# Feed-forward output: the last six inner tiles of output tiles 2 to 5 as two pairs of seven products

## What is computed

```python
def rms_norm(x, g):
    y = x * lax.rsqrt(jnp.mean(x * x, axis=-1, keepdims=True) + EPS)
    return y * g

def half_swiglu(x, g, w_in, w_out):
    a, b = jnp.split(rms_norm(x, g) @ w_in, 2, axis=-1)
    return x + 0.5 * ((jax.nn.silu(a) * b) @ w_out)

for i in range(2):
    x = half_swiglu(x, norm_w[i, 0], w_ffn_in[i, 0], w_ffn_out[i, 0])
    x = x + mixer(rms_norm(x, norm_w[i, 1]))     # state space, then attention
    x = half_swiglu(x, norm_w[i, 2], w_ffn_in[i, 1], w_ffn_out[i, 1])
y = rms_norm(x, norm_f)
```

## Time and profile before

| | us |
|---|---|
| median of 3 runs | 2453.65 (2452.84 to 2457.1) |
| the profiled execution, its own time | 2449.32 |
| its span in the trace | 2447.5 |
| PE busy | 2414.4 (99% of the span) |
| DVE busy | 1837.7 (75%) |
| ACT busy | 1392.9 (57%) |
| POOL busy | 755.4 (31%) |

### The profile page before, as it was taken

The page is one execution under the profiler, slowest core; times in us unless marked ns, Lnnn a source line. Parts: engine busy times, 40 slices in busy tenths (PEclk is TensorE's granted clock), DMA queues, the critical chain, the costliest instruction groups (busy, mean ns, idle before and its releaser), DMA issues.

```text
span 2447.5 us, 50261 instructions
## 1 busy us (share of the span) xinstructions
PE 2414.4 (99%) x19713; PEld 2362.0 (97%) x19713; DVE 1837.7 (75%) x3054; ACT 1392.9 (57%) x2388; POOL 755.4 (31%) x739
## 2 busy tenths in 40 slices
PE   8999999999999999999999999999999999999998
PEld 8999999999999989999999999999999998999998
DVE  8979766977777788978876988875235438988875
ACT  7757553545555556757666766664223227767663
POOL 1222224545555542222223222224322321222222
PEclk9999999999999999999999999999999999999999
DMA  6677753133333325676765677764433434677762
GB/s 192 162 170 166 171 118 111 49 103 106 106 106 97 106 83 147 152 177 160 175 139 137 150 172 162 172 148 134 158 131 122 136 110 111 158 172 162 174 149 88
DMA packets 105686, 339.01 MB, mean 139 GB/s; under 512 B 13776, under 2 KB 17360, under 8 KB 87184
## 3 DMA queue, kind: packets, MB, share of 16 engines
q1 hardware_dynamic: 53936, 242.40, 30.0%
q0 software_dynamic: 51552, 93.87, 22.8%
HBM read 223.06 MB, written 19.32 MB: 99 GB/s over the span
## 4 chain that ended last, share of the span: by engine, by line
PE 94%; DVE 4%; ACT 1%; issue 1%; DMA 0%; SPq 0%; POOL 0%; DVEq 0%; ACTq 0%
PE ps L1644 17%; PE ps L1642 17%; PE ps L1652 17%; PE ps L1540 7%; PE ps L1548 7%; PE ps L1541 7%; PE ps L1661 2%; PE ps L1662 2%; PE ps L1669 2%; PE ps L1591 1%; PE ps L1581 1%; PE ps L1582 1%; PE ps L1980 1%; PE ps L1982 1%; PE ps L1981 1%; DVE sb_acc L2713 1%
## 5 line engine op out<-in xcount | busy, mean ns | idle before, releaser
L1644 PE MATMUL ps<-sb_ual,sb_hw 128*128 128x288 f32 x2240 | 614.2, 296 | 0.0
L1642 PE MATMUL ps<-sb_uah,sb_hw 128*128 128x288 f32 x2240 | 610.7, 295 | 0.1
L813 POOL DMA_DIRECT2D sb_lw<-sb_rawf x328 | 282.3, 866 | 961.6 <-ACT sb_lw L987 944.8
L1642 PEld LDWEIGHTS ps<-sb_uah,sb_hw 128*128 128x128 f32 x2240 | 421.0, 188 | 0.7 <-issue 0.5
L1644 PEld LDWEIGHTS ps<-sb_ual,sb_hw 128*128 128x128 f32 x2240 | 421.2, 188 | 0.0
L796 POOL TENSOR_TENSOR sb_wl<-sb_raw,sb_wh 128x512 fp32r<-128x512 f32 (+1 forms) x170 | 282.4, 1678 | 389.8 <-ACT sb_wh L956 377.3
L1652 PE MATMUL ps<-sb_uah,sb_lw 128*128 128x288 f32 x2240 | 385.0, 294 | 0.0
L1540 PE MATMUL ps<-sb_uh,sb_wh 128*128 128x288 f32 x1360 | 373.6, 301 | 0.1
L1541 PE MATMUL ps<-sb_ul,sb_wh 128*128 128x288 f32 x1360 | 366.8, 296 | 0.0
L1652 PEld LDWEIGHTS ps<-sb_uah,sb_lw 128*128 128x128 f32 x2240 | 328.3, 188 | 0.7 <-DVE sb_lw L2336 0.4
L1540 PEld LDWEIGHTS ps<-sb_uh,sb_wh 128*128 128x128 f32 x1360 | 255.7, 188 | 7.6 <-issue 5.0
(11 more groups left out here) (366 smaller groups left out, 5096.3 us busy)
## 6 DMA issues: line engine op xcount, KB each, us to landing
sb_lw<-sb_rawf POOLq DMA_DIRECT2D x358, 256.0 KB, 3.7
sb_rawf<-w_ffn_in SPq DMA_DIRECT2D x87, 1024.0 KB, 5.0
sb_rawf<-w_ffn_so SPq DMA_DIRECT2D x32, 1024.0 KB, 5.0
sb_raw<-w_ssd SPq DMA_DIRECT2D x64, 512.0 KB, 3.6
sb_raw<-w_att SPq DMA_DIRECT2D x40, 512.0 KB, 3.7
sb_rawf<-w_ffn_out SPq DMA_DIRECT2D x32, 384.0 KB, 3.1
sb_h<-state SPq DMA_DIRECT2D x8, 1024.0 KB, 5.1
ssm_sample<-sb_h SPq DMA_DIRECT2D x8, 1024.0 KB, 4.8
```

Of the source, the lines that this page charges most:

```text
L813: pool.dma_start(slot(lw, p), rawf[:, s % 2, i * BL:(i + 1) * BL], accum_op=ALU.add).then_inc(ld_in[i], 16)
L1642: pe.matmul(out, w[:, k * P:(k + 1) * P], high[k], start=begins and k == 0, stop=False, skip_group_check=True)
L1644: pe.matmul(out, w[:, k * P:(k + 1) * P], low[k], start=False, stop=False, skip_group_check=True)
```

## The change

The unit count of a stage grows from 30 to 32: units E0 = 30 and E1 = 31 do the last six inner tiles for the output tiles 2 and 3 (E0) and 4 and 5 (E1) by sevens, with 3 pairs of inner tiles instead of 4, so 9 matmuls a product. The output tiles 0, 1, 6 and 7 stay plain. PE's order is: tiles 0 and 1, the products of E0 and E1, tile 6 (with product 4 of E1 behind its first two blocks), tile 7. The inner tiles 16 to 21 get their sums of halves (`h_side3`, `h_sides`, `high_hs`, `low_hs` with 3 sides of 288 columns, and `high_s4_out`, `low_s4_out` for the fourth). The weights of E0 and E1 come in two transfers of 768 KB. All work on the scaled tiles of the next stage stands behind product 7 of E1 in DVE's list, for the tiles in the order 0, 1, 3, 2, 5, 4, and only then comes `add_out(6)`.

```diff
-NU = 30
+NU = 32
+OUT_TILES = (0, 1, 6, 7)
+END_SLOT = {1: 3, 5: 4, 6: 5, 2: 6, 3: 0, 7: 1, 4: 2}
+LAST = 29
+E0, E1 = 30, 31
+ORDER = (0, 1, 3, 2, 5, 4, 6, 7)
...
+        def tile_done(f, m):
+            if m in OUT_TILES:
+                return x_done, OUTS * f + OUT_TILES.index(m) + 3
+            return x_part, UPDATED[f * NU + E0 + m // 2 - 1, 7 if m % 2 else 4]
...
+                if n >= E0:
+                    sp.wait_ge(wl_done, U_FFN[f] + n - E0 + 1)
+                    dst = rawf[:, s % 2, :].rearrange("p (b c) -> p b c", b=4)[:, :, 0:KO // 2 * P]
+                    sp.dma_start(dst, io["w_ffn_se"][f, n - E0]).then_inc(blk_in[s % 2], 16)
+                    return
...
@@ scalar engine: ffn @@
-                silu(last)
-                high_h(last)
-                high_out(f, 2)
+                direct(last + 1, 1)
+                silu(last)
+                high_h(last)
+                high12(last + 1)
+                direct(last + 1, 2)
+                high_hs(f, 2, 2)
+                direct(last + 1, 3)
+                high_s4_out(f)
+                high34(last + 1)
+                for i, m in enumerate(ORDER):
+                    if i == 0:
+                        direct(last + 2, 1)
+                        direct(last + 2, 2)
+                        high12(last + 2)
+                        direct(last + 2, 3)
+                        high34(last + 2)
+                        high_out(f, 2)
+                        high_out(f, 3)
...
@@ tensor engine: full @@
                 if n == 0 and part == 0 and f == 2:
-                    pe.wait_ge(x_done, KD * f - 1 + 2)
+                    pe.wait_ge(*tile_done(1, 6))
...
@@ tensor engine: ffn @@
                 first_outs(f)
-                for m in range(2, KD - 1 if f == 3 else KD):
-                    out(f, m)
+                for p in (1, 2, 5, 6, 3, 7):
+                    times(s, p)
+                times(s + 1, 1)
+                times(s + 1, 5)
+                times(s, 4)
+                times(s + 1, 6)
+                times(s + 1, 2)
+                times(s + 1, 3)
+                times(s + 1, 7)
+                out_highs(f, 6, range(2))
+                times(s + 1, 4)
+                out_highs(f, 6, range(2, KO))
+                out_lows(f, 6, range(KO)).then_inc(unit_done, 1)
+                if f < 3:
+                    out(f, 7)
...
@@ vector engine: ffn @@
                 gate_half(last)
+                diff1(e)
                 hidden(last)
+                diff2(e)
                 low_h(last)
+                diff34(e)
+                h_sides(f, 2, 2)
+                low12(e)
+                low_hs(f, 2, 2)
+                low_s4_out(f)
+                diff1(e1)
+                diff2(e1)
-                for m in range(KD - 1 if f == 3 else KD):
-                    add_out(m)
...
+                add_product(e, 1)
+                add_out(0)
+                add_out(1)
+                add_product(e, 2)
+                add_product(e, 5)
+                low34(e)
+                add_product(e, 6)
+                diff34(e1)
+                low12(e1)
+                add_product(e, 3)
+                add_product(e, 7)
+                add_product(e1, 1)
+                add_product(e1, 5)
+                add_product(e, 4)
+                add_product(e1, 6)
+                low34(e1)
+                add_product(e1, 2)
+                add_product(e1, 3)
+                add_product(e1, 7)
+                next_sides(0)
+                add_product(e1, 4)
+                next_sides(1)
+                next_sides(3)
+                next_sides(2)
+                next_sides(5)
+                next_sides(4)
+                add_out(6)
+                if f == 1:
+                    add_out(7)
+                next_sides(6)
+                if f < 3:
+                    if f != 1:
+                        add_out(7)
+                    next_sides(7)
```

More of the change, by code:

```diff
@@ L110, in update_order @@
     for f in range(4):
-        for i in OPENING:
+        for i in OPENING[0:2]:
             u = f * NU + i
@@ L116, in update_order @@
             yield from ((u + 3, 7), (u + 3, 4))
+        u = f * NU + E0
+        yield from ((u, p) for p in (1, 2, 5, 6, 3, 7))
+        yield from ((u + 1, 1), (u + 1, 5), (u, 4), (u + 1, 6), (u + 1, 2), (u + 1, 3), (u + 1, 7), (u + 1, 4))
 DONE = {key: i + 1 for i, key in enumerate(product_order())}
@@ L627, in ffn @@
             def ffn(f):
-                for n in range(NU):
+                for n in range(E0):
                     if n < 2 and f:
@@ L640, in ffn @@
                         store_samples(GROUPS - 1)
-                for m in range(KD):
+                for m in OUT_TILES[0:2]:
+                    out_unit(f, m)
+                for n in (E0, E1):
+                    blocks(f * NU + n)
+                for m in OUT_TILES[2:]:
                     out_unit(f, m)
@@ L812, in add_direct @@
                 pool.wait_ge(nd_done, nth_negative(s, p))
-                pool.dma_start(slot(lw, p), rawf[:, s % 2, i * BL:(i + 1) * BL], accum_op=ALU.add).then_inc(ld_in[i], 16)
+                pool.dma_start(slot(lw, s, p), rawf[:, s % 2, i * BL:(i + 1) * BL], accum_op=ALU.add).then_inc(ld_in[i], 16)
             def ffn(f):
-                for n in range(NU):
+                for n in range(E0):
                     s = f * NU + n
@@ L1210, in ffn @@
                 full_units(f)
-                for n in range(FULL, NU):
+                for n in range(FULL, E0):
                     s = f * NU + n
@@ L1235, in ffn @@
                         high_full(2 * NU, 1)
-                    act.wait_ge(x_done, KD * f + m + 2 + 1)
+                    act.wait_ge(*tile_done(f, m))
                     if f == 3 and m == 1:
                         act.wait_ge(prod_done, DONE[last, 4])
-                        for i, y in enumerate((y0, y1)):
-                            nc.scalar.activation(y[:, :], x[:, i, :], ACT.Copy,
-                                                 scale=gains[:, last_norm, one(i)]).then_inc(y_scaled, 1)
+                        for i2, y in enumerate((y0, y1)):
+                            nc.scalar.activation(y[:, :], x[:, i2, :], ACT.Copy,
+                                                 scale=gains[:, last_norm, one(i2)]).then_inc(y_scaled, 1)
                     if f == 1:
@@ L1532, in product @@
                 pe.wait_ge(wh_done, u + 1)
-                for k in range(nk):
+                order = range(nk) if chunk is None else [m - ORDER[chunk % KD] // 4 * 4 for m in ORDER[chunk % KD:chunk % KD + nk]]
+                for i, k in enumerate(order):
                     if between and k == at:
@@ L1565, in full @@
                 if n == 0 and part == 0 and f == 2:
-                    pe.wait_ge(x_done, KD * f - 1 + 2)
+                    pe.wait_ge(*tile_done(1, 6))
                 if part == 1 and n == 1:
                     pe.wait_ge(sqrt_ready, NORM_OF_FFN[f] + 1)
-                for m in range(KD):
+                for i, m in enumerate(ORDER if f == 2 and n == 0 and part == 0 else range(KD)):
                     if part == 0 and n == 1 and m == KD // 2:
@@ L1629, in times @@
                     pe.wait_ge(s_ready, 5 * f + 5)
-                if opening and p in (1, 2):
+                if n == E0 and p == 3:
+                    pe.wait_ge(hs_ready, nth_split(f, 2, 3) + 1)
+                if opening and p in (1, 2) and n < E0:
                     pe.wait_ge(h_ready, TILES * f + 8 * c + (7 if p == 1 else 8))
                 if n in FAST_OUT:
-                    high, low = ([h[:, k, SIDE[p], :] for k in range(4)] for h in (hh, hl))
+                    high, low = ([h[:, 3, at + k, :] if n >= E0 and p == 3 else h[:, k, SIDE[p], :] for k in range(pairs)]
+                                 for h, at in ((hh, 4), (hl, 0)))
                 else:
                     high, low = ([a[:, SIDE[p], k, :] for k in range(4)] for a in (uah, ual))
-                w, v, out = slot(hw, p), slot(lw, p), ps[:, bank, 0:HALF]
-                for k in range(4):
+                w, v, out = slot(hw, s, p), slot(lw, s, p), ps[:, bank, 0:HALF]
+                for k in range(pairs):
                     if n == FULL and p == 5:
@@ L1650, in times @@
                     pe.wait_ge(lt12_done if p > 4 and p < 7 else lt34_done, e + 1)
-                for k in range(4):
+                for k in range(pairs):
                     ins = pe.matmul(out, v[:, k * P:(k + 1) * P], high[k], start=False,
-                                    stop=k == 3, skip_group_check=True)
+                                    stop=k == pairs - 1, skip_group_check=True)
                 ins.then_inc(prod_done, 1)
@@ L3241, in laid_out @@
     w_out = []
+    w_end = []
     for i in range(2):
```

240 lines of the change are left out of this document (144 added, 96 removed).

## The result

The changed kernel takes 2474.45 us (median of 4 runs, 2473.10 to 2475.38), the kernel before 2453.24 beside it (2451.41 to 2457.10): ratio **1.0088, 95% interval 1.0075 to 1.0101**, slower by 21.2 us where 11.9 were forecast. That lies 1.5 us over the forecast's own range (2458 to 2473) and inside the range with the rivals (2456 to 2476). The profiled executions differ by 2475.38 - 2449.32 = 26.1 us, since the one of after lies 0.9 over its median and the one of before 3.9 under.

A forecast was written before the change was run, and what follows sets the result against it. PE was taken to bound the kernel, busy 2414.4 of 2447.5 us. Terms -10.8 + 9.0 + 1.8 + 9.9 + 2.0 = +11.9 on 2449.32 gave 2461.2, or 2465.5 on the median's scale; range 2458 to 2473, with rivals 2456 to 2476.

The forecast's parts named there:

- Step 5, stage 1: Ahead of stage 2, PE stands 9.9 us for DVE's list of scaled tiles behind product 7; bounds 8 to 12.
- Step 6, the clock: Behind the stand ahead of stage 2, the granted clock falls once to its lower level, costing 2.0 us.
- Step 1: Output tiles 2 to 5: 14 products of 9 matmuls save PE 2.7 us a stage, 10.8 in four.
- Step 4: In the pairs, PE waits on DVE at products 6, 3 and 7: 2.25 us a stage, 9.0 in four.
- step 2: Inner units 25 to 29: DVE's added work costs nothing but one low part, about 1.0 us; last `gate_half` 353.06 to 353.9.
- The rival of the clock in the pairs: Clock falls in the pairs too, 1.4 us in each of four stages: +5.6, 2471.1 us; chance 0.2.
- step 5 for stages 0, 2 and 3: Scaled tiles behind product 7 delay what follows: 0.5 us each in stages 0 and 2, 0.8 more in 2; sum 1.8.
- The other rivals: Pairs don't wait, 2456.6 us, chance 0.12; neither wait exists, 2444.7, 0.05; PE saves nothing, +20 and more, 0.03.

The follow-up runs named there:

- run 1: Changed kernel with the sums of halves, their low parts and casts between stages 1 and 2 on 8 columns instead of 256: 2468.03 us, ratio 1.0061.
- run 2: Changed kernel with the additions of output tiles 6 and 7 moved up DVE's list in stage 1: 2472.25 us, ratio 1.0082.
- run 11: run 6 with the small sums of run 1 (8 columns instead of 256): 2460.99 us, ratio 1.0030.
- run 8: Changed kernel with scaled work of output tiles 0 and 1 moved between the second pair's products in stage 1 alone: 2473.30 us, ratio 1.0086.
- run 7: Changed kernel with 66 added, unused matmuls on PE in the stand ahead of stage 2: 2471.32 us, ratio 1.0084.
- run 4: Changed kernel with tile 7's addition directly behind tile 6's in stages 0 and 2, and the mixer weights' cast earlier: 2470.70 us, ratio 1.0073.
- run 5: Changed kernel with squares of output tiles 0 and 1 and their additions moved between the second pair's products in stage 3 alone: 2471.53 us, ratio 1.0084.
- run 3: Changed kernel with DVE's additions of products ahead of weight differences and output additions in each stage's first pair: 2472.53 us, ratio 1.0081.
- run 6: Changed kernel with the orders of run 2, run 3 and run 4, and the first two tiles early in stages 0, 2 and 3: 2463.47 us, ratio 1.0047.
- run 9: run 6 with stage 1's first two tiles early too: 2467.90 us, ratio 1.0062.
- run 10: run 6 with 44 added, unused matmuls on PE in the stand ahead of stage 2: 2465.41 us, ratio 1.0058.

## Why the prediction was right, and where it was short

- **Step 5, stage 1: right.** 9.9 us forecast, 9.4 measured; 6.15 a pair, 6.01 measured. Runs 1, 2 and 11 show that it is the amount of DVE's work behind product 7, and run 8 that the pair has hardly room to take it back (0.6 us of 4.6, by one profile each).
- **Step 6, the clock: right in its cause.** 2.0 forecast; stage 2 is 2.5 longer in the ledger, and run 7, which shows that the stand causes the fall, gives 1.3 back. The Trainium skill (TensorE: Matmul & The Clock Gate, section "HAM oscillation — how this bites in real kernels") says that a burst behind a wait for input starts at the lower clock. The rows of after agree for the stand of 9.4 us; behind the short waits of the pairs it came so in 6 stage ends of 28 (below).
- **Step 1: right in its count, not in its effect.** 72 matmuls less, products at 1.19 us (1.18 forecast), two tiles at 4.76 each. Stage ends still came out 0.70 and 0.76 longer, not shorter.
- **Step 4: mis-sized.** 1.05 + 0.9 + 0.3 = 2.25 was forecast a stage; 1.58 + 0.82 + 0.36, with 0.2 at the smaller ones 3.0, is what stage 0 shows. It isn't a matter of this execution: in the 28 stage ends of the seven profiles with this order in the first pair (after and runs 1, 2, 4, 5, 7, 8), PE stands 1.35 to 1.42 us at product 6, and DVE's addition of product 1 ends 16.1 to 16.4 us behind `first_outs`, where the forecast's times give 15.6. The slip begins in step 2, which moved the last `gate_half` by 0.84 us: in after it begins 4.87 us behind `first_outs`, in before 2.89, so it came 1.98 later. Step 2 counted one low part of 1.0 us there. Two instructions ahead of it, that ran beside POOL's low part (346.78 to 350.64), took 2.15 and 2.39 us, where instructions of these sizes take 0.45 and 0.76 a few us on. The rest of the chain takes some of it back, 0.7 is left at the addition of product 1. Four stages: 3 us more.

```profile
346.80 2.15 DVE L2539 TENSOR_TENSOR sb_hr<-sb_he 128x288 f32<-128x288 f32 x1
348.87 2.39 DVE L2513 TENSOR_TENSOR sb_hl<-sb_he,sb_hh 128x576 fp32r<-128x576 f32 x1
...
357.11 0.76 DVE L2513 TENSOR_TENSOR sb_hl<-sb_ge,sb_hh 128x576 fp32r<-128x576 f32 x1
```

- **The rival of the clock in the pairs: came true in part.** In those same 28 stage ends, with the same waits, the clock fell in the first pair in 6: stage 3 of after, stage 0 of run 2, stage 1 of runs 4 and 8, stages 0 and 2 of run 5. Each fall cost 1.0 to 1.2 us (1.4 forecast): stage 0's end is 41.77 and 41.86 us long with it and 40.5 to 40.7 without. So the same code goes either way from one execution to the next, and a forecast can only give it a chance. Stage 3's pairs in after:

```profile
2428.00:2432.00 4.00, 2.35 (x16) 1.91 (x15) 3.96 (x8) 2.59 (x6) 1.72 (x2) 1.00 0.67 106
2432.00:2436.00 4.00, 3.71 (x17) 3.73 (x18) 4.00 (x6) 2.01 (x3) 0.01 (x1) 0.58 0.89 193
```

- **The step that failed is step 5 for stages 0, 2 and 3.** It priced the delay of scaled tiles to the first matmul of what follows, 1.8 us, where the ledger has +3.8 in the mixer, +2.8 in the attention and +6.2 in the tail. It stopped at the first wait. Behind `add_out(6)` there stand ScalarE's cast of the next weights and tile 7, 1.4 and 1.5 us (run 4), and behind stage 3's product 7 seven squares pass one at a time through one buffer to the last sums (run 5). Step 5 had the 1.5 us of a square in stages 0 and 2, and didn't apply it to stage 3, whose end is the kernel's end. Shown of it are 3.9 us in the tail, 1.8 in the attention (0.8 of them priced) and 0.6 in the mixer: 5.5 of the 14.2 that the ledger has over the forecast. The slip of the pairs is 3 more, the falls of the clock in stage 3's pair and in the attention 2.1. For most of what remains, above all in the mixer, the cause stays open.
- **Luck.** The total fell inside the wider range through terms that the forecast didn't have; the rival that was to account for such a time, the clock falling in all four stages' pairs, came true in one.
- **The other rivals are out.** No wait is missing, and PE saved what the diff said.

## What to carry to other kernels

When a change makes PE's work less and puts the helper engines' work behind it, sum the whole list that is queued after the last product, on every engine, for each place where the kernel goes on, the end of the kernel too; the first wait is only its beginning. A wait's releaser names the last instruction of a list: moving that one alone cuts the stand in two and gives nothing back (run 2). Work put back between products helps only as far as the helper engine is idle there: in stage 1 it hardly was (run 8), in stage 3 the two squares fitted and gave 3.9 us (run 5).

## What the chip did that I had not expected

- POOL's accumulating transfers don't land in a fixed time. The one for product 1 of E1 in stage 1, issued 15.6 to 15.8 us behind `first_outs` everywhere, landed after 4.7 to 5.6 us in the seven profiles with after's order and after 6.76, 3.57, 7.36, 6.39 and 4.87 us in runs 3, 6, 9, 10 and 11. At 6.39 us and more PE waited for it, at 5.58 it didn't. Only kernels with run 3's order show the long ones, but not each time; the cause isn't shown.
- The clock fell behind a stretch of 4 us with 2.35 us of PE work as well as behind an empty one, but not behind one with 2.01 in stage 0 of after. Busy time in a stretch alone doesn't tell which waits cost the clock.

```profile
364.00:368.00 4.00, 2.01 (x15) 1.00 0.63 110
368.00:372.00 4.00, 3.89 (x28) 1.00 0.82 185
```
